# Hybrid encoder block: the window group's q projection as seven products of half-sized blocks, k behind it

## The reference

```python
h = rmsnorm(x, norm_mix[l])
proj = jnp.einsum('bsd,dc->bsc', h, w_in[l])          # 1024 tokens x 1024 -> 2464 columns
qa, ka, va, ga, cq, ckv, kr, gb = jnp.split(proj, split_idx, axis=-1)
ya = window_attention(qa, ka, va, attn_sink[l])       # qa: 512 columns, ka and va: 128 each
ya = ya * jax.nn.silu(ga)                             # ga: 512 columns
q = einsum(rmsnorm(cq, q_a_norm[l]), w_uq[l])         # latent group, 8 heads of 64 + 32 (rope)
kv = einsum(rmsnorm(ckv, kv_a_norm[l]), w_ukv[l])
yb = latent_attention(...) * jax.nn.silu(gb)
x = x + einsum(concatenate([ya, yb]), w_out[l])
out = rmsnorm(x, final_norm)
```

## Time and profile before

| | us |
|---|---|
| three timed runs, median (lowest, highest) | 608.26 (607.14, 610.05) |
| the profiled execution, its own time | 607.01 |
| its span, first to last instruction | 605.2 |
| TensorE busy in it | 594.2 (98%) |
| VectorE, ScalarE, GpSimd busy | 446.7, 356.4, 293.3 |
| mean granted TensorE clock | 0.997 of full |

### The profile page before, as it was taken

How to read it: one execution, slowest core, us unless ns; L and a number is a source line. 1 busy time by engine, 2 the same in 40 slices (tenths; PEclk the granted TensorE clock), 3 DMA queues, 4 the chain that set the end, 5 groups by cost and what they waited for, 6 DMA issues and landing times.

```text
span 605.2 us, 9197 instructions
## 1 busy us (share of the span) xinstructions
PE 594.2 (98%) x3076; PEld 483.1 (80%) x3076; DVE 446.7 (74%) x802; ACT 356.4 (59%) x762; POOL 293.3 (48%) x273
## 2 busy tenths in 40 slices
...
GB/s 254 189 282 223 134 158 249 191 278 165 242 252 231 231 69 1 36 1 36 2 27 113 247 148 183 191 179 191 188 171 205 195 135 179 175 387 328 1 172 108
DMA packets 72431, 102.11 MB, mean 169 GB/s; under 512 B 10232, under 2 KB 43008, under 8 KB 72384
## 3 DMA queue, kind: packets, MB, share of 16 engines
...
## 4 chain that ended last, share of the span: by engine, by line
PE 91%; DVE 3%; ACT 2%; DMA 2%; issue 1%; POOL 1%; SPq 0%; ACTq 0%
PE ps L1823 18%; PE ps L1825 17%; PE ps L1824 17%; PE ps L2117 9%; PE ps L2095 7%; PE ps L2025 5%; PE ps L2030 5%; PE ps L1995 3%; PE ps L2045 2%; PE ps L2005 2%; PE ps L1982 2%; PE ps L1981 2%; PE ps L2006 2%; DMA lat_scratch<-lat_b 1%; DMA wn_raw<-w_in 1%
## 5 line engine op out<-in xcount | busy, mean ns | idle before, releaser
L1673 DVE TENSOR_TENSOR pT_lo<-ps,pT_hi 128x512 fp32r<-128x512 f32 x102 | 69.3, 683 | 21.5 <-ACT pT_hi L1236 20.3
L1823 PE MATMUL ps<-hT_hi,w_hi 128*128 128x512 f32 x208 | 84.0, 404 | 0.0
L1825 PE MATMUL ps<-hT_hi,w_lo 128*128 128x512 f32 x208 | 81.4, 391 | 0.0
L1824 PE MATMUL ps<-hT_lo,w_hi 128*128 128x512 f32 x208 | 81.0, 390 | 0.0
L1223 ACT ACTIVATE p_b<-ps,stat 128x1024 f32<-128x1024 f32 x64 | 71.3, 1115 | 12.5 <-DVE stat L1648 12.1
L1648 DVE TENSOR_REDUCE stat<-ps 128x1 f32<-128x1024 f32 x64 | 76.5, 1211 | 2.2 <-PE ps L2045 2.0
L1236 ACT ACTIVATE pT_hi<-ps 128x512 fp32r<-128x512 f32 x102 | 60.4, 596 | 23.9 <-PE ps L2095 23.6
L2095 PEld LDWEIGHTS ps<-ident,p_b 128*128 128x128 f32 x408 | 48.8, 140 | 17.4 <-issue 5.2
L2095 PE MATMUL ps<-ident,p_b 128*128 128x128 f32 x408 | 62.0, 275 | 0.6 <-DVE pT_lo L1673 0.3
L809 POOL TENSOR_SCALAR p_w<-p_w,stat 128x384 f32<-128x384 f32 (+1 forms) x40 | 24.4, 622 | 55.6 <-DVE stat L1556 55.6
L925 POOL TENSOR_TENSOR pT_lo<-p_land,pT_hi 128x512 fp32r<-128x512 f32 x26 | 33.4, 1291 | 30.4 <-ACT pT_hi L1243 30.4
...
## 6 DMA issues: line engine op xcount, KB each, us to landing
w_raw<-w_in SPq DMA_DIRECT2D x13, 512.0 KB, 4.5
...
p_land<-probs_scratch SPq DMA_DIRECT2D x13, 512.0 KB, 4.5
x_in<-x SPq DMA_DIRECT2D x8, 512.0 KB, 3.8
wt_raw<-w_out SPq DMA_DIRECT2D x8, 512.0 KB, 4.5
t_scratch<-wt_hi SPq DMA_DIRECT2D x16, 256.0 KB, 2.5
t_scratch<-wt_lo SPq DMA_DIRECT2D x16, 256.0 KB, 2.6
q<-q_h SPq DMA_DIRECT2D x16, 256.0 KB, 3.6
```

The source lines that it names most:

```text
L1673: nc.vector.tensor_tensor(pT_lo[at_], ps[:, 4 + a, :].rearrange("p (k c) -> p k c", c=P), f(pT_hi[at_]), ALU.subtract).then_inc(s_bTl, 1)
L1823: nc.tensor.matmul(o, a_hi, b_hi, start=first, stop=False, skip_group_check=goes_on)
L1824: nc.tensor.matmul(o, a_hi, b_lo, start=False, stop=False, skip_group_check=goes_on)
L1825: return nc.tensor.matmul(o, a_lo, b_hi, start=False, stop=last, skip_group_check=goes_on)
```

## The change

The q projection (512 columns x 1024 tokens x 1024 channels) is cut into halves on all three sides. Block (b, c) of h is channel half b, token half c (`h_block`); block (a, b) of the weights is column half a, channel half b (`wq`). Seven products of such blocks or of sums of them take the place of eight. Each is 2 banks x 4 tiles x 3 matmuls = 24 matmuls of 128x512 (`q_product`), in the order P1, P2, P3, P6, P7, P4, P5. P2 adds to the banks of P1, P7 to those of P6.

- Weights: two loads of 1 MB (`load_wq`) in the places of the loads of m = 0 and m = 1. POOL makes four sums of 128x1024 and seven splits of 128x1024 (a high and a low instruction each), two slots as before.
- h: DVE makes the sums of blocks with ten instructions of 128x2048 (`h_add`), all linked. Six of them stand in the loop of the up jobs, after the second rope pair (job 13) and ahead of the v jobs; two and two stand between the products. Each of the four sums is then split in pieces of 128x512: four on ACT (`h_sum_hi`), four on DVE (`h_sum_lo`).
- Results: ACT keeps P1 (`keep_p1`), DVE adds up `u2`, `u3` and six bank sums, and the eight q blocks are emptied with two pieces of 64x512 on ACT and on DVE each (`q_block_hi`, `q_block_lo`), as before.
- `M_COLS` now has q first and k at m = 4, `gated` begins at g = 8, and the sums of `w_out` move to m = 4, 5, 6, 7 and g = 8, 10, 12, 13.
- P1, P3 and P6 wait for the up jobs' banks: P1 for banks 2 and 3, which up jobs 24 and 25 (v) used last.

The diff, cut to its core:

```diff
+        wq_raw = [at(f"wq_raw{a}", kb, [P, KT, 2 * P]) for a, kb in enumerate((115, 142.5))]
+        wq_sum = at("wq_sum", 150.5, [P, 4, 2 * P])
...
-        M_COLS = [KA] + [QA + P * i for i in range(4)] + [GA + P * i for i in range(4)] \
+        M_COLS = [QA + P * i for i in range(4)] + [KA] + [GA + P * i for i in range(4)] \
             + [GB + P * i for i in range(4)]
         NM = len(M_COLS)
         N_WIN_JOB = 2 * (NM - 5)
+        MQ = 4
...
+        QP1, QP2, QP3, QP6, QP7, QP4, QP5 = range(7)
+        QT_OF = {QP6: 1, QP7: 0, QP4: 1, QP5: 0}
+        QT_ORDER = (QP7, QP6, QP4, QP5)
+        Q_BANK = {QP1: 2, QP2: 2, QP3: 4, QP6: 6, QP7: 6, QP4: 2, QP5: 4}
+        Q_BLOCKS = ((0, 0, 0, 2), (0, 0, 1, 3), (1, 0, 0, 2), (1, 0, 1, 3),
+                    (1, 1, 0, 0), (1, 1, 1, 1), (0, 1, 0, 4), (0, 1, 1, 5))
+        Q_SUMS = (0, 0, 2, 2, 3, 5, 6, 6)
...
-        WT_POOL, WT_PARTS = (2, 3, 5, 6), (3, 6, 9, 11)
+        WT_POOL, WT_PARTS = (4, 5, 6, 7), (8, 10, 12, 13)
...
+            def load_wq(a):
+                if a == 0:
+                    sp.wait_ge(s_uq, 1)
+                else:
+                    sp.wait_ge(s_latT, NT)
+                    sp.wait_ge(s_up, 8)
+                sp.dma_start(wq_raw[a][:, :, :],
+                             w_in[:, QA + 2 * P * a:QA + 2 * P * (a + 1)].rearrange("(k p) c -> p k c", p=P)) \
+                    .then_inc(s_w[a], 16)
             def load_w(m):
-                if m >= 2:
-                    sp.wait_ge(s_wr, m - 1)
-                elif m == 0:
-                    sp.wait_ge(s_uq, 1)
+                sp.wait_ge(s_wr, N_SPLIT + m - 1 if m >= MQ + 2 else QP6 + 1)
                 sp.dma_start(w_raw[:, m % 2, :, :],
                              w_in[:, M_COLS[m]:M_COLS[m] + P].rearrange("(k p) c -> p k c", p=P)) \
...
-            load_w(2)
-            load_w(3)
             load_wt(0)
             load_w(4)
+            load_w(5)
+            load_w(6)
             load_wt(1)
+            load_w(7)
             store_wt(0)
-            load_w(5)
             load_wt(2)
-            load_w(6)
+            load_w(8)
             store_wt(1)
-            load_w(7)
             load_wt(3)
             store_wt(2)
-            load_w(8)
             store_wt(3)
...
+            def split_wq(n, raw):
+                if n >= 2:
+                    wait_q_product(pool, n - 2, 1)
+                s = (n + 1) % 2
+                split(raw, w_flat(w_hi, s), w_flat(w_lo, s), s_wh, n + 1, s_wr)
...
+            pool.wait_ge(s_w[0], 16)
+            pool.wait_ge(s_up, N_Q)
+            split_wq(QP1, wq(0, 0))
+            split_wq(QP2, wq(0, 1))
+            pool.wait_ge(s_w[1], 16)
+            nc.gpsimd.tensor_tensor(sq1, wq(1, 0), wq(1, 1), ALU.add).then_inc(s_wts, 1)
+            nc.gpsimd.tensor_tensor(wq(1, 0), wq(0, 0), wq(1, 0), ALU.subtract).then_inc(s_wts, 1)
+            pool.wait_ge(s_wts, 1)
+            nc.gpsimd.tensor_tensor(wq(0, 0), sq1, wq(0, 0), ALU.subtract).then_inc(s_wts, 1)
+            pool.wait_ge(s_wts, 3)
+            nc.gpsimd.tensor_tensor(wq(0, 1), wq(0, 1), wq(0, 0), ALU.subtract).then_inc(s_wts, 1)
+            pool.wait_ge(s_wts, 4)
+            split_wq(QP3, wq(0, 1))
+            split_wq(QP6, wq(0, 0))
+            split_wq(QP7, wq(1, 0))
+            split_wq(QP4, wq(1, 1))
+            split_wq(QP5, sq1)
+            for m in range(MQ, NM - 3):
                 split_w(m)
                 if m in WT_POOL:
                     sums_wt(WT_POOL.index(m))
...
+            def h_sum_hi(n):
+                o, raw = ht_hi[QT_OF[QT_ORDER[n]]], h_t1 if QT_ORDER[n] == QP5 else h_t3
+                act.wait_ge(s_qt, NT + (1, 3, 4, 2)[n])
+                if n == 0:
+                    act.wait_ge(s_up, len(UP))
+                elif n >= 2:
+                    wait_q_product(act, (QP6, QP7)[n - 2], 1)
+                for k in range(4):
+                    nc.scalar.activation(o[:, k, :], raw[:, k, :], ACT.Copy).then_inc(s_qth, 1)
+            def q_block_hi(n):
+                a, c, i, bank = Q_BLOCKS[n]
+                if n < 2:
+                    wait_q_product(act, QP2, i)
+                else:
+                    act.wait_ge(s_qc, NT + Q_SUMS[n])
+                for q in range(2):
+                    h = 4 * a + 2 * i + q
+                    last = nc.scalar.activation(q_st[0:HD, h, c * HALF:(c + 1) * HALF], ps[HD * q:HD * (q + 1), bank, :],
+                                                ACT.Copy, scale=-A_SCALE / SLOPE[h])
+                last.then_inc(s_ga, 1)
+            h_sum_hi(0)
+            keep_p1(0)
+            keep_p1(1)
+            q_block_hi(0)
+            h_sum_hi(1)
+            q_block_hi(1)
+            h_sum_hi(2)
+            h_sum_hi(3)
+            for n in range(2, 8):
+                q_block_hi(n)
...
             lat_lo(NT - 1)
+            def h_add(o, x, y, op, last=False):
+                ins = nc.vector.tensor_tensor(o[:, :, :], x, y, op)
+                if last:
+                    ins.then_inc(s_qt, 1)
+                else:
...
+                if kind == "r" and t == 1 and h == 1:
+                    h_add(h_t3, h_block(hT_hi, 1, 1), h_block(hT_hi, 0, 1), ALU.subtract)
+                    h_add(h_t3, h_t3[:, :, :], h_block(hT_lo, 1, 1), ALU.add)
+                    h_add(h_t3, h_t3[:, :, :], h_block(hT_lo, 0, 1), ALU.subtract, True)
+                    h_add(h_t1, h_block(hT_hi, 0, 1), h_block(hT_hi, 0, 0), ALU.subtract)
+                    h_add(h_t1, h_t1[:, :, :], h_block(hT_lo, 0, 1), ALU.add)
+                    h_add(h_t1, h_t1[:, :, :], h_block(hT_lo, 0, 0), ALU.subtract, True)
...
+            def h_sum_lo(n):
+                i = QT_OF[QT_ORDER[n]]
+                raw = h_t1 if QT_ORDER[n] == QP5 else h_t3
+                if n == 1:
+                    wait_all_stored(dve)
+                for k in range(4):
+                    dve.wait_ge(s_qth, NT + 4 * n + k + 1)
+                    nc.vector.tensor_tensor(ht_lo[i][:, k, :], raw[:, k, :], f(ht_hi[i][:, k, :]),
+                                            ALU.subtract).then_inc(s_qtl, 1)
+            def q_block_lo(n):
+                a, c, i, bank = Q_BLOCKS[n]
+                cols = slice(c * HALF, (c + 1) * HALF)
...
+                        op1=ALU.subtract)
+                last.then_inc(s_ge, 1)
+            def u2(i):
+                wait_q_product(dve, QP6, i)
+                dve.wait_ge(s_qu3, NT + i + 1)
+                link(nc.vector.tensor_tensor(q_u2[i][:, :], ps[:, Q_BANK[QP6] + i, :], q_u3[i][:, :], ALU.add))
+                nc.vector.tensor_tensor(q_u2[i][:, :], ps[:, Q_BANK[QP3] + i, :], q_u2[i][:, :],
+                                        ALU.add).then_inc(s_qu2, 1)
+            def u3(i):
+                wait_q_product(dve, QP7, i)
+                nc.vector.tensor_tensor(q_u3[i][:, :], ps[:, Q_BANK[QP7] + i, :], q_u3[i][:, :],
+                                        ALU.add).then_inc(s_qu3, 1)
+            def q_block_sum(bank, src, u):
+                nc.vector.tensor_tensor(ps[:, bank, :], ps[:, src, :], u[:, :], ALU.add).then_inc(s_qc, 1)
+            h_sum_lo(0)
+            dve.wait_ge(s_qtl, NT + 4)
+            h_add(h_t3, h_t3[:, :, :], h_block(hT_hi, 0, 0), ALU.add)
+            h_add(h_t3, h_t3[:, :, :], h_block(hT_lo, 0, 0), ALU.add, True)
+            q_block_lo(0)
+            h_sum_lo(1)
+            dve.wait_ge(s_qtl, NT + 8)
+            h_add(h_t3, h_block(hT_hi, 1, 0), h_t3[:, :, :], ALU.subtract)
+            h_add(h_t3, h_block(hT_lo, 1, 0), h_t3[:, :, :], ALU.add, True)
+            q_block_lo(1)
+            u2(0)
+            u2(1)
+            h_sum_lo(2)
+            u3(0)
+            u3(1)
+            h_sum_lo(3)
+            dve.wait_ge(s_qu3, NT + 4)
+            for i in range(2):
+                wait_q_product(dve, QP4, i)
+                q_block_sum(Q_BANK[QP4] + i, Q_BANK[QP4] + i, q_u3[i])
+            q_block_lo(2)
+            dve.wait_ge(s_qu2, NT + 2)
+            for i in range(2):
+                if i == 0:
+                    wait_q_product(dve, QP5, 0)
+                else:
+                    dve.wait_ge(s_g, 2 * MQ)
+                q_block_sum(i, Q_BANK[QP5] + i, q_u3[i])
+                q_block_sum(Q_BANK[QP5] + i, Q_BANK[QP5] + i, q_u2[i])
+            for n in range(3, 8):
+                q_block_lo(n)
+            for g in range(2 * MQ, N_WIN_JOB):
                 evac_g(g)
...
+                    if m == MQ:
+                        pe.wait_ge(s_qu3, NT + 3 + g % 2)
                     else:
...
+            def q_product(n, block=None):
+                s = (n + 1) % 2
+                pe.wait_ge(s_wr, n + 1)
+                for i in range(2):
+                    o = ps[:, Q_BANK[n] + i, :]
+                    if n in (QP1, QP3, QP6):
+                        wait_up_copied(pe, UP_LAST[Q_BANK[n] + i])
+                    elif n == QP2:
+                        pe.wait_ge(s_qu3, NT + i + 1)
```

(30 more changed lines are left out.)

78 lines of the change are left out of this document (45 added, 33 removed).

## The result

| | before | after |
|---|---|---|
| median of 4 runs (lowest, highest), us | 607.87 (607.14, 610.05) | 628.54 (625.09, 629.50) |
| profiled execution, its own time, us | 607.01 | 628.54 |
| its span, us | 605.2 | 626.8 |
| mean granted TensorE clock | 0.997 | 0.986 |

The ratio is 1.033 (95% interval 1.030 to 1.036): 20.7 us slower. The forecast was 623, so its sign holds, and so does its mechanism up to the last product; 5.5 us of loss are more than it said, and about half of the whole loss stands behind the products, where it had put 1.6.

The account below looks back on a forecast made before the run. PE was taken as the bound (matmul in flight 594.2 of 605.2 us). -5.44 + 9.2 + 2.0 + 1.0 + 5.7 + 2.0 + 1.6 = +16.1 on 607.0 gave 623.1, stated as 623, range 617 to 631.

Parts of the forecast that it names:

- its mechanism: Around the q products: DVE's and POOL's SBUF instructions exclude each other, so PE waits and its clock falls.
- The forecast for the sums: In the q products: wait before P1 9.2, clock 2.0, wait before P3 1.0, wait before P7 5.7, clock 2.0.
- 24 matmuls, -5.44: On PE: eight gated jobs of 24 matmuls become seven products, at unchanged pitch, saving 5.44 us.
- The turns: Ahead of P1: DVE's six sums alternate with POOL's whole instructions, so PE starts P1 at 141.1, 9.2 us late.
- The clock: Behind PE's gaps before P1 and P7: falls to 1.2 GHz, costing 2 us each; bounds 0 and 5.4 for the first.
- P3's weights: Before P3: POOL's low part ends at 155.0, P2 at 154.0, so PE waits 1.0 us for weights.
- `u2(0)` before P7: Before P7: DVE, in turns with POOL, finishes `u2(0)` at 171.55; P6 ends at 165.9, so PE waits 5.7 us.
- Behind the products, 1.6: After P5: k pieces 0.4, late evacuation for g = 11 0.7, split for g = 12 0.5; together 1.6, bounds 0 and 4.
- the first: Rival, ahead of P1: DVE and POOL pass each other, the added work is hidden, 603.2 us; chance 0.11.
- The second: Rival, before P1 and P7: only part of the turns bites, 614.4 us if only the first wait stays; chance 0.21.
- third: Rival, before P1: a gap there alone, with a full clock, cancels the gain, 604 to 610 us; chance 0.05.

Follow-up runs that it names:

- number 6: Kernel before, no products, with q first, the changed `w_out` places and SyncE order, and block 9's load ahead of the last `w_out` store: 617.1 us, ratio 1.014.
- number 10: Kernel after with block 9's load early, eight of ten h sums and GpSimd's four weight sums cut short, P5's weights another block: 611.1 us, ratio 1.006.
- number 5: Kernel after with the load of weight block 9 issued ahead of the last store of `w_out`: 626.6 us, ratio 1.030.
- number 1: Kernel after with GpSimd's four weight sums cut to 8 columns and P5 given an unsummed weight block: 623.5 us, ratio 1.027.
- number 2: Kernel after with four of VectorE's six early h sums cut to 8 elements a partition: 618.0 us, ratio 1.019.
- number 3: Kernel after with the last v job computed seven times, to keep PE busy through its first wait: 629.2 us, ratio 1.037.
- number 4: Kernel before, no products, with q first, k behind, and the changed places of the `w_out` sums and SyncE's loads: 617.1 us, ratio 1.016.
- number 11: Kernel after, later high parts on ScalarE, block 9's load early, last `w_out` part at g = 14: six h sums cut, 612.5; sums whole, P5's late, 621.2.

## Why the prediction was right, and where not

The runs split the loss, in medians, and in one trace of each, counted from the start of the second rope pair to the end of the span, which leaves out what ran ahead of the change:

| part | medians | us | traces | forecast |
|---|---|---|---|---|
| places of `w_out` and SyncE's order | number 6 less before: 617.15 - 607.89 | +9.3 | +7.8 | +1.6 |
| the seven products | number 10 less number 6: 611.14 - 617.15 | -6.0 | -3.5 | -5.4 |
| nearly all sums of h and weights | number 5 less number 10: 626.58 - 611.14 | +15.4 | +14.2 | +19.9 |
| block 9's load, late | after less number 5: 628.54 - 626.58 | +2.0 | +2.5 | 0 |
| sum | | +20.7 | +21.0 | +16.1 |

Each part is what it costs in this order of steps; other orders were not run. The forecast for the sums is 9.2 + 2.0 + 1.0 + 5.7 + 2.0. Step by step:

- *24 matmuls, -5.44.* Right: 24 fewer, at the same pitch. Number 10 against 6 gives -6.0, with some 3 us of noise to each side, and -3.5 in the traces, where number 10's waits behind the products are longer (0.9 and not 0 for `k_lo`, 5.9 and not 5.1 for `Y`). That the median lies so near to 5.44 is luck.
- *The turns.* Right, and shown from both sides by numbers 1 and 2. The forecast had VectorE's six sums end at 139.2 and PE start at 141.1; they ended at 138.8 and 140.75. The single sum was put at 2.25 and takes 2.29. The wait came to 8.10 and not 9.2: PE started P1 0.35 earlier, its up jobs ran 0.57 later, and 0.16 is the way in which idle time is counted. The Trainium skill's rule that the prediction names ("SBUF — State Buffer", section "Who interferes with whom") agrees with 4.4 against 2.29 and with 0.20 against 2.25.
- *The clock.* Taken as 2 twice, without a row for how long it stays low: 1.99 and 1.9. That the size is right is luck, since the bounds were 0 and 5.4. It fell a third time (1.6), which wasn't foreseen.
- *P3's weights.* 1.0 forecast, 0.77 measured.
- *`u2(0)` before P7.* 5.7 forecast, 2.54 measured: right place, too large. The step that failed is the order of turns in "`h_add`, POOL high, wait: DVE to 164.1": the forecast had GpSimd ready at 160.5 and VectorE at 160.8, so that both GpSimd parts of P7's split stood ahead of VectorE's second sum. In the trace the split starts when P3 frees its slot, at 160.22, and VectorE's sum had begun at 159.79. So only the high part came between the two sums (2.29 and 3.02), the low part of 2.4 fell behind them, and `q_u2` ended at 168.0, not 171.55; the rest is that VectorE came there 1.0 earlier. In number 3, where the splits for P3 and P6 come closer together, P6 and P7 lose 4.8 in waits where the kernel after lost 2.5. So who comes first by half a microsecond moves some 2 us here; no run tested that alone.
- *Behind the products, 1.6.* This is the term that was mis-sized, and by far the most: 10.2 in the trace (0.42 + 0.43 at g = 10 and 12, near the forecast 0.4 and 0.5, while the 0.7 at g = 11 did not come; then 2.11, 5.66 and 1.6 of clock, which it did not have), and +9.3 and +10.0 by numbers 6 and 4. The prediction ended its walk at g = 12 with "from there PE has the same work and its slack as before". It priced what VectorE and GpSimd add in the moved steps, but not that the last part, moved from g = 11 to 13, stands next to two consumers of another kind: the emptying of the last bank that the gate jobs need (job 16), and on SyncE the load of block 9, which is issued in written order behind four pairs of stores and the k loads. GpSimd's list has that split ahead of the window probabilities. SyncE's queue was to be read past the place where the change ends.
- *Rivals.* Numbers 1 and 2 exclude the first (the engines don't pass each other). The second and third fall with the trace: the load landed at 124.16, as taken (124.1). The forecast came near in part by luck, because two errors partly cancel: against it, by the medians, the sums cost 4.5 less and the products 0.6 less, the tail 9.7 more (9.3 + 2.0 - 1.6). That is 4.6, and the profiled execution of before, from which 623 was reckoned, lay 0.9 under the median.

What stays open: why the last versions (number 11) lose 6 us more than their expectation; their waits were read, but not their turns one by one. The same code ahead of the change took up to 4 us more in one profiled execution than in another (the second rope pair began at 109.0 in number 10, 110.9 in the kernel after, 112.8 in number 6 and 113.2 in number 2), so differences of 1 us between two of these runs prove nothing.
